# Delta rule with diagonal blocks of 32 rows, decay rows by turns on TensorE, and a new order of the front's steps

## The reference

```python
z = _rmsnorm(x, norm1_w) @ w_in           # q|k|v|gate|beta|decay of the delta rule, q|k|v of the attention
qkv = silu(causal_conv4(z[qa, ka, va]))   # 4 heads x 128
qa, ka = l2norm(qa) * 128 ** -0.5, l2norm(ka)
g = -exp(a_log) * softplus(alpha + dt_bias); gc = cumsum(g)      # within a chunk
decay = exp(gc[i] - gc[j]) for i >= j
m = I + strictly_lower((k * beta) @ k.T * decay)
u, w = triangular_solve(m, [v * beta, k * beta * exp(gc)])
# per chunk: v_new = u - w @ S;  o = (q * exp(gc)) @ S + (q @ k.T * decay) @ v_new;  S = S * exp(gc_last) + k_dec.T @ v_new
ob = dilated_attention(qb, kb, vb, rel_bias)                     # 8 heads x 64, three branches
h = x + concat(gated_norm(o), ob) @ w_out
out = h + moe(_rmsnorm(h, norm2_w))       # top 4 of 32 experts, 1024 -> 2048 -> 1024
```

## Time and profile before

| | us |
|---|---|
| median of 3 runs (lowest, highest) | 1085.33 (1084.62, 1086.16) |
| span of the profiled execution | 1083.5 |
| TensorE busy | 1019.8 (94%) |
| VectorE busy | 303.6 (28%) |
| ScalarE busy | 164.3 (15%) |
| HBM read and written | 427 MB, 394 GB/s over the span |
| mean granted clock of TensorE | 0.990 |

### The profile page before, as it was taken

How to read it: one execution, slowest core, us unless ns; L and a number is a source line. 1 busy time by engine, 2 the same in 40 slices (tenths; PEclk the granted TensorE clock), 3 DMA queues, 4 the chain that set the end, 5 groups by cost and what they waited for, 6 DMA issues and landing times.

```text
span 1083.5 us, 12842 instructions
## 1 busy us (share of the span) xinstructions
PE 1019.8 (94%) x5096; PEld 447.5 (41%) x5096; DVE 303.6 (28%) x703; ACT 164.3 (15%) x283; POOL 21.3 (2%) x37
## 2 busy tenths in 40 slices
PE   9999999999999999989999989988999898988898
PEld 7888866333434343434344323232333332223232
DVE  4987754312222222222322111101111111111111
ACT  3513436011111111111001000000111011111101
POOL 3201000000000000000000000000000000000000
PEclk9999999999999999999999999999999999999999
DMA  9724779999999999999999999999999999999997
GB/s 324 283 83 161 279 287 365 405 425 428 425 419 432 434 432 428 432 432 429 428 432 428 427 429 431 431 432 429 431 431 431 431 431 430 431 431 434 425 424 289
DMA packets 39036, 427.64 MB, mean 395 GB/s; under 512 B 8251, under 2 KB 10524, under 8 KB 20188
## 3 DMA queue, kind: packets, MB, share of 16 engines
q1 hardware_dynamic: 37840, 426.84, 93.9%
q10 hardware_dynamic: 1164, 0.34, 0.1%
HBM read 424.42 MB, written 2.75 MB: 394 GB/s over the span
## 4 chain that ended last, share of the span: by engine, by line
PE 50%; DMA 41%; DVE 5%; issue 1%; ACT 1%; SPq 1%; ACTq 0%; DVEq 0%
DMA store<-in_w_gate_up_dram 24%; PE bank L2312 17%; DMA store<-in_w_down_dram 16%; PE bank L2370 13%; PE bank L1789 5%; PE bank L1781 3%; PE bank L2218 2%; PE bank L1916 2%; PE bank L2077 2%; PE bank L2283 1%; DVE flow L1627 1%; PE bank L2335 1%; DVE flow L1620 1%; ACT flow L1010 1%; DVE flow L1625 1%
## 5 line engine op out<-in xcount | busy, mean ns | idle before, releaser
L2312 PE MATMUL bank<-store,flow 128*64 128x512 f32 x2048 | 452.0, 598 | 13.9 <-DMA store<-in_w_gate_up_dram 12.9
L2312 PEld LDWEIGHTS bank<-store,flow 128*64 128x64 f32 x2048 | 145.9, 138 | 314.1 <-issue 289.9
L2370 PE MATMUL bank<-store,flow 128*64 128x512 f32 x992 | 228.1, 610 | 32.1 <-DMA store<-in_w_down_dram 20.5
L1620 DVE TENSOR_SCALAR flow<-bank 128x512 f32<-128x512 f32 x32 | 22.1, 692 | 607.8 <-PE bank L2312 607.8
L2370 PEld LDWEIGHTS bank<-store,flow 128*64 128x64 f32 x992 | 74.0, 140 | 165.5 <-issue 138.4
L1010 ACT ACTIVATE flow<-flow 128x512 f32<-128x512 f32 x32 | 20.2, 630 | 445.0 <-DVE flow L1620 445.0
L2227 PE MATMUL bank<-qkT 64*128 64x512 f32 x248 | 61.9, 616 | 0.0
L1026 ACT COPY qkT<-bank 128x512 f32<-128x512 f32 x31 | 18.2, 586 | 194.6 <-PE bank L2370 194.6
L1020 ACT COPY flow<-flow 128x512 f32 x30 | 33.7, 1124 | 27.5 <-DVE flow L1695 11.2
L2227 PEld LDWEIGHTS bank<-qkT 64*128 64x128 f32 x248 | 21.2, 186 | 40.1 <-issue 40.1
L1781 PE MATMUL bank<-store 128*128 128x256 f32 x160 | 35.5, 381 | 0.0
(11 more groups left out here) (360 smaller groups left out, 671.0 us busy)
## 6 DMA issues: line engine op xcount, KB each, us to landing
store<-in_w_gate_up_dram SPq DMA_DIRECT2D x50, 4096.0 KB, 26.9
store<-in_w_down_dram SPq DMA_DIRECT2D x57, 2048.0 KB, 20.9
store<-in_w_gate_up_dram SPq DMA_DIRECT2D x26, 2048.0 KB, 13.8
store<-in_w_in_dram SPq DMA_DIRECT2D x6, 2048.0 KB, 13.7
store<-in_w_down_dram SPq DMA_DIRECT2D x9, 1024.0 KB, 25.0
store<-in_w_out_dram SPq DMA_DIRECT2D x1, 4096.0 KB, 14.3
store<-in_w_gate_up_dram SPq DMA_DIRECT2D x3, 1024.0 KB, 7.2
flow<-in_w_down_dram SPq DMA_DIRECT2D x1, 2048.0 KB, 11.9
```

The source lines that it names most:

```text
L1620: dve.tensor_scalar(gt, bank[4][:], LIMIT, None, ALU.min).then_inc(g_min, 1)
L2312: ins = mm(dst[SLOTS * hf:SLOTS * (hf + 1), :], rows[:, c:c + SLOTS], store[:, slot_at(j, odd) + c0:slot_at(j, odd) + c0 + 512], start=fir ...
L2370: ins = mm(dst[SLOTS * hf:SLOTS * (hf + 1), :], turned[:, c:c + SLOTS], w[:, hf * 512:(hf + 1) * 512], start=f == 0, stop=f == KT - 1)
```

## The change

- Diagonal blocks of 32 rows: `n_cols` and `t_cols` have 32 columns a head, the masks follow. Each of the 32 blocks is loaded four times, to 128 partitions; every partition inverts the two 16x16 halves on its diagonal (`invert_halves`, step J0), and then (`join_halves`, step J1) picks the four columns of the halves that are its own, and computes the lower left part as a product of the two inverses and the block's lower left.
- The series has the powers of D up to the third: stage Q, the product X and ScalarE's copy in stage 7, and the product Y and its copy in stage 8 are gone. Stages 8 and 9 of tile 1 use bank 6 and not bank 4.
- The decay rows are the column of the cumulative decay, broadcast as the stationary operand and turned by the identity, one turn a head. `ug` and its eight instructions are gone; TensorE waits for the cumulative decay itself.
- The first tap of each convolution is a scaled copy on ScalarE (`first_tap`) behind its `evac`. The first convolution stands before the decay's inputs, the sums of x before the decay; the quarter sums of piece 4 go to GpSimd and those of piece 3 to VectorE; the sixth convolution and q's sums are now steps V6 and Q0 of the order, behind 01 and 11, and `g5` stands in front.
- A new order.

```diff
-FINE = 16
-BLOCKS = 64
+FINE = 32
+HALF = FINE // 2
+BLOCKS = 32
+PARTS = 4
...
-BY_POOL = {3: 3}
-SUMMED_BY = {("b", 3): ("sums", 0), ("d", 3): ("sums", 1), ("b", 4): ("sums", 2), ("c", 4): ("sums", 3),
+BY_POOL = {4: 3}
+SUMMED_BY = {("b", 3): ("sums", 1), ("c", 3): ("sums", 2), ("d", 4): ("sums", 3),
...
-    text = ("01 11 a3 a4 b3 b4 g5 u5 c3 c4 h5 J0 d3 d4 r0 12 e4 02 0E e3 1E r1 a5 r2 n0 17 07 f0 b5 f1 f2 g6 "
-            "08 f3 c5 S0 d5 09 S1 P0 0A P1 e5 S2 h6 T0 0B a6 u6 O0 0Q P2 b6 0C T1 S3 c6 O1 1K T2 d6 P3 0M e6 "
-            "s0 S4 O2 18 P4 0N T3 W0 T4 19 O3 1A 0D O4 S5 P5 1B W1 T5 1Q O5 w0 X0 1C X1 W2 1M A0 1N H0 H1 R0 "
-            "1D L0 W3 F0 X2 G0 M0")
+    text = ("g5 01 11 Q0 V6 a3 a4 b3 b4 h5 J0 c3 c4 d3 d4 J1 e4 e3 r0 r1 u5 r2 a5 0E 1E 02 n0 b5 12 17 07 f0 f1 08 "
+            "c5 f2 f3 09 S0 d5 0A S1 P0 g6 e5 0B S2 P1 h6 T0 0C a6 u6 O0 1K T1 P2 b6 O1 S3 18 c6 T2 P3 19 d6 O2 1A "
+            "e6 s0 0M S4 T3 P4 1B W0 0N O3 1C T4 S5 P5 0D O4 W1 1M T5 w0 X0 1N O5 X1 A0 W2 1D H0 H1 R0 W3 L0 F0 X2 "
+            "G0 M0")
...
-            sp.dma_start(n_sq, by_block(n_dram)).then_inc(ld_blocks, 16)
+            sp.dma_start(n_sq, bass.AP(n_dram.tensor, 0, [[0, PARTS], [FINE * FINE, BLOCKS], [1, FINE * FINE]])
+                         ).then_inc(ld_blocks, 16)
             sp.wait_ge(t_ready, 1)
-            sp.dma_start(by_block(t_dram), t_sq).then_inc(st_scratch, 16)
+            sp.dma_start(bass.AP(t_dram.tensor, 0, [[PARTS * FINE, PARTS], [FINE * FINE, BLOCKS],
+                                                    [HALF * FINE, 2], [1, PARTS * FINE]]),
+                         t_own.rearrange("q (a n) -> q a n", a=2)).then_inc(st_scratch, 16)
...
+            def first_tap(u):
+
+                act.wait_ge(z_evac, evacuated(u))
...
+                for c in (CONV_AT[u], CONV_AT[u] + 1):
+                    tp.mark(act.activation(conv[:, c, :], zpad[:, c, 0:S], ACT.Copy, scale=cw[:, 0, c:c + 1]))
...
-            def invert_blocks():
+            def invert_halves():
 
                 dve.wait_ge(ld_blocks, 16)
...
+                for j in range(1, HALF - 1):
+                    shape = [P, 2, j, HALF - 1 - j]
+                    part = t_new[:, 0:2 * j * (HALF - 1 - j)].rearrange("q (a c r) -> q a c r", a=2, c=j)
+                    st.step(dve.tensor_tensor(part, n_diag[:, :, j + 1:HALF, j].unsqueeze(2).to_broadcast(shape),
+                                              t_of[:, :, 0:j, j].unsqueeze(3).to_broadcast(shape), ALU.mult))
+                    st.step(dve.tensor_tensor(t_of[:, :, 0:j, j + 1:HALF], t_of[:, :, 0:j, j + 1:HALF], part,
+                                              ALU.add))
+
+            def join_halves():
...
+                def product(rows, cols):
+                    shape = [P, PARTS, HALF, HALF]
+                    part = t_new.rearrange("q (c r k) -> q c r k", c=PARTS, r=HALF)
+                    st.step(dve.tensor_tensor(part, rows.unsqueeze(1).to_broadcast(shape),
+                                              cols.unsqueeze(2).to_broadcast(shape), ALU.mult))
+                    return part
+
+                st.mark(dve.memset(own_second[:, :, 0:HALF], 0.0))
+                picked = own_halves.rearrange("q (a m) -> q a m", a=2)
+                st.step(dve.tensor_scalar(picked, columns(0), part_of[:, 0:1], None, ALU.mult))
+                for g in range(1, PARTS):
+                    st.step(dve.scalar_tensor_tensor(out=picked, in0=columns(g), scalar=part_of[:, g:g + 1],
+                                                     in1=picked, op0=ALU.mult, op1=ALU.add))
+                st.mark(dve.tensor_copy(own_diag, own_halves.rearrange("q (a c r) -> q a c r", a=2, r=HALF)))
+                first = own_halves[:, 0:PARTS * HALF].rearrange("q (c r) -> q c r", r=HALF)
+                st.step(dve.reduce_sum(low_right, product(n_low, first), AX_X))
+                Tally(dve, t_ready).mark(dve.reduce_sum(
+                    own_first[:, :, HALF:], product(t_of[:, 1].rearrange("q k r -> q r k"), low_right), AX_X))
...
                     elif s == 8:
-                        st.step(dve.tensor_copy(m["F"], Y[:]))
-                        gdn.mark(dve.tensor_copy(m["V"], Z[:]))
+                        gdn.mark(dve.tensor_copy(m["V"], W[:]))
...
+            pe.wait_ge(gap_ready, 1)
             for t in range(T):
 
-                pe.wait_ge(ug_ready, HG * (t + 1))
-                gr.mark(mm(bank[t][:], ones[:], ug[:, t, :], start=True, stop=True))
+                for h in range(HG):
+                    ins = mm(bank[t][:, h * P:(h + 1) * P], gd[:, 5, t, h:h + 1].to_broadcast([P, P]), ident[:],
+                             start=True, stop=True, is_transpose=True)
+                gr.mark(ins)
...
                     elif s == 7:
-                        product(X, m["G"], m["L"])
                         ins = product(Y, m["L"], m["G"])
...
                     elif s == 8:
-                        product(Y, m["N"], m["D"])
-                        ins = product(Z, m["G"], m["H"])
+                        ins = product(W, m["G"], m["H"])
```

More of the change, by code:

```diff
@@ L91 @@
 ORDER = attention_order()
-PE_STAGES = {1, 2, 7, "K", 8, 9, 10, 11, "Q", 12, 13}
+PE_STAGES = {1, 2, 7, "K", 8, 9, 10, 11, 12, 13}
 DVE_STAGES = PE_STAGES | {"E", "M", "N"}
-ACT_STAGES = {7, "M", "N"}
+ACT_STAGES = {"M", "N"}
 EARLY_STAGES = {1, 2, 7}
-BANK4_STAGES = {2, 8, 9}
-BANK4 = [step for step in ORDER if (step[0] == "gdn" and step[2] in BANK4_STAGES) or step[:2] == ("a", 6)]
+BANK4_STAGES = {(0, 2), (1, 2), (0, 8), (0, 9)}
+BANK4 = [step for step in ORDER if (step[0] == "gdn" and step[1:] in BANK4_STAGES) or step[:2] == ("a", 6)]
 BANK7 = [step for step in ORDER if step[0] in "TO"]
@@ L1202, in _ @@
             convolve(1)
+            dve.wait_ge(ba_psum, 1)
+            dve.wait_ge(ld_small, 16 * 8)
+            ba = bank[3][:, 0:T * 2 * HG].rearrange("p (t n) -> p t n", t=T)
+            st.mark(dve.tensor_scalar(gd[:, 4], ba[:, :, 0:HG], -1.0, None, ALU.mult))
+            dd.mark(dve.tensor_tensor(gd[:, 3], ba[:, :, HG:2 * HG],
+                                      gd[:, 1, 0].unsqueeze(1).to_broadcast([P, T, HG]), ALU.add))
+            dd.mark(dve.tensor_scalar(col[:, 17:18], col[:, 17:18], DH ** -0.5, None, ALU.mult))
+            sums_of_x()
             dve.wait_ge(dec_act, 2)
@@ new lines, in join_halves, with columns @@
+            def join_halves():
+                def columns(g):
+                    return t_of[:, :, PARTS * g:PARTS * (g + 1), :].rearrange("q a c r -> q a (c r)")
+                def product(rows, cols):
[15 more added lines that the diff above has]
+                    own_first[:, :, HALF:], product(t_of[:, 1].rearrange("q k r -> q r k"), low_right), AX_X))
@@ L1357, in _ @@
                 if kind == "J":
-                    invert_blocks()
+                    (join_halves if a else invert_halves)()
+                    continue
+                if kind == "V":
+                    convolve(a)
+                    continue
+                if kind == "Q":
+                    Tally(dve, q_sums).step(picked_sums(2, gd[:, 9]))
+                    st.step(dve.tensor_scalar(gd[:, 9], gd[:, 9], EPS, EPS * DK * DK, ALU.add, ALU.mult))
                     continue
@@ L2069, in _, with product @@
                         pe.wait_ge(z_sum, sums_done("e", 5))
[L2070 removed]
+                    if (t, s) == (1, 12):
                         pe.wait_ge(z_evac, evacuated("d6"))
                     take_shared((kind, t, s))
[L2074 removed]
+                    def product(dst, lhsT, rhs):
                         for h in range(HG):
```

136 lines of the change are left out of this document (62 added, 74 removed).

## The result

The changed kernel takes 1109.88 us (median of 4 runs, 1108.75 to 1112.6) where the kernel before took 1085.07 in the same session: a ratio of 1.0229, 95% interval 1.0214 to 1.0245. It is slower, as forecast, but by 24.8 us where 9.2 were forecast, and it lies outside the range (1083 to 1100).

What follows compares the result with a forecast made beforehand. TensorE bounds the front, streamed bytes the rest. Seven waits of 17.2 us, less 6.2 of removed TensorE work, 1.8 of small gaps and 0.1, give 9.2 on 1085.3: 1094.5 us, range 1083 to 1100.

Steps and rivals of the forecast that it cites:

- removed work decides: Rival: VectorE keeps up, waits stay under 6.2 us and TensorE's removed work makes it faster, 1079.1 us; chance 0.16.
- The DMA hides it: Rival: the DMA is already short of time at 160 to 180 us, late block 0 costs nothing, 1085.3; chance 0.08.
- the first trip: Loading the blocks through DRAM ahead of J0, four times the bytes: 0.8 us more, ends 0 and 3.
- The second trip: Storing the inverses and loading their columns after J1: nothing added to the time of before.
- (1): ScalarE's last silu waits for VectorE's sixth convolution and q's sums behind 01 and 11, delaying b3: 1.6 us.
- (2): TensorE waits before stage 02, listed behind 0E, which needs the inverse's columns, back at 91.5: 2.7 us.
- (3): Stage 12 stands behind n0 on VectorE, so stage 17 starts late, and f1 and S0 wait for copies: 2.4 us.
- (4): Before stage 0C, VectorE needs 7.9 us for its steps since 0A while TensorE has 4.5 of work: 3.2 us.
- (5): T1 waits for O0, which stands behind a6's copy and u6: 1.2 us.
- (6): 0M stands behind s0, so VectorE starts S4 late and O3, 1C and T4 come late: 2.4 us.
- (7): W1 needs the bank that 0D empties, queued on VectorE behind P5, which needs ScalarE's exps: 3.7 us.
- The clock: Rival: TensorE's clock falls behind idle gaps at two waits, 1.2 us or a little more each, 1097; chance 0.17.

Runs made afterwards that it cites:

- loads: The changed kernel with the load that replicates the blocks four times split into four transfers of 32 partitions; 1103.94 us (ratio 1.0164).
- twos: The changed kernel with the load of the blocks as two transfers of two copies each; 1113.62 us (ratio 1.025).
- best5: As hold, with step h5 moved behind r2 and c5 put between f0 and f1; 1086.99 us (ratio 1.0008).
- pool: As loads, with GpSimd's four squares held until the end of J1; 1101.44 us (ratio 1.0148).
- straight: As pool, with the second half inverse copied once so J1's second product reads no strided operand; 1102.53 us (ratio 1.0149).
- trips: As loads, with the store of the inverses also split into four transfers of 32 partitions; 1103.1 us (ratio 1.016).
- late: The changed kernel with three steps moved earlier in the list (g6 ahead of 09, 0M ahead of e6, 0D ahead of S5); 1097.77 us (ratio 1.011).
- hold: As best3, with the copy of straight and two weight loads held until the columns' load has landed; 1087.39 us (ratio 1.0016).
- only0d: The changed kernel with one step moved, 0D ahead of S5; 1102.85 us (ratio 1.015).
- warm: The changed kernel with 59 dummy products of the unit matrix put into three of TensorE's idle times; 1104.46 us (ratio 1.0169).
- best3: The changed kernel with the edits of loads, pool and late, u6 behind O0, and 02, 12, b5, u5 placed anew around the inverse; 1089.29 us (ratio 1.0027).

## Why the prediction was right or wrong

**The sign and the mechanism** were right. The waits that VectorE's order makes for TensorE decide, and the later start of block 0 (206.1 for 183.2) arrives in the total, with 1.9 us more on top. The rival "removed work decides" fell: idle time in the front was 21.5 us, not under 6.2. "The DMA hides it" fell too.

**The steps up to 69 us** were right to 0.4: the last projection unit ends 0.7 earlier (0.75 forecast), blocks leave at 64.35 (64.0), b3 starts at 68.9 (68.7).

**The term that failed first is the first trip** ("0.8 more for the first trip, ends 0 and 3"). It was priced by its bytes; it took 6.5 more (8.7 for 2.1). 4.6 of them come from an access pattern whose outer dimension of four engaged four engines (loads, twos): split, the same bytes took 4.1 (best5). J0 began at 75.2, not 70.7. The kernel's rows before gave no price for this shape; but its outer dimension could have been counted, and the Trainium skill's page named under twos has the rule, which the prediction did not draw on. With the load split, J0 starts at 70.70 as forecast.

**J0** was 9.2 for 8.8, **J1** 8.6 for 6.8. Without GpSimd beside it (1.3) and the strided operand (0.7) J1 would be 6.6 (pool, straight); the rows it was priced by had neither. **The second trip** took 5.7 for 4.5; its store has an outer dimension of four too, but splitting it won nothing (trips).

**The waits by their numbers**, forecast and found: (1) 1.6 and 1.57; (2) 2.7 and 7.82, with e4's 2.34 beside it, which the list had not foreseen; (3) 2.4 and 1.22; (4) 3.2 (its own terms, 7.9 less 4.5, give 3.4) and 2.67; (5) 1.2 and 0.87; (6) 2.4 and 1.59; (7) 3.7 and 3.44. Waits 4 to 7, 10.5 by forecast, were 8.6; late took 7.2 of them away and left T1, T4 and 0.16 at 0C. The whole miss of wait 2 is the inverse's.

**The clock** was the second step that failed: the sum puts it at nothing, and a rival adds 2.4 us for it. It came on top: three falls, 1.7 to 2.7 us each instead of 1.2, together 6.3. It should have been a term of the sum: the forecast had three waits of 2.7 and more, and the row it cited, a wait of 2.76, had the fall behind it. The Trainium skill's "TensorE: Matmul & The Clock Gate", section "HAM oscillation", says that a long enough gap in TensorE's work throttles it, so that the next products start cold. The trace agrees for the three long waits (2.67 to 7.82 us).

**The sum at X1**: forecast 9.3 later, found 22.9. The difference of 13.6 is 4.3 of waits (21.5 less 17.2), 6.3 of clock, and 3.0 that the prediction has under small gaps. Of these 1.8 is its third wrong term: it took off 1.8 us of gaps in the kernel before, and that trace has 0.4 us of them (PE busy 96.92 us, in the columns of the earlier trace rows):

```profile
57.28:154.60 97.32, 96.92 (x589) 79.84 (x586) 69.35 (x150) 31.47 (x73) 4.46 (x4) 1.00 0.55 204
```

The other 1.2 lies in how a wait is read. The modelled ends of products overlap the next row, so each of the eleven waits costs 0.07 to 0.17 us more from start to start than the idle time in its bracket; T1 starts 2.03 us behind the row before it, where that step took 0.99 before, and its bracket says 0.87.

**What the change could have given.** 6.2 us less TensorE work is real (the decay rows' share was seen, 0.9). Against it stands a chain of trip, J0, J1 and trip that takes 29.1 us (hold) to 35.2 (the changed kernel) from the blocks' store to the columns where it took 18.5 before (67.0 to 85.53). Covered as well as any list tried covers it, it leaves TensorE idle for about what was saved (5.3 us in hold, whose X1 starts at 154.65 for 154.60), and the time is that of the kernel before.

## What to carry to other kernels

Where a change puts a new transfer on a chain, count the outermost dimension of its pattern before its bytes: one transfer with four copies as its outer dimension took 8.7 us where four transfers of 32 rows took 4.1. Where the order of work is one list for all engines, look for steps on a helper engine that stand just ahead of what TensorE needs, and give each long wait a second term for the slow products behind it, which in the changed kernel came to 1.7 to 2.7 us a wait. Measure such a list with single moves: the one measured alone here was worth 7.0 us and the three together 12.1, where the arithmetic that the change removed is 6.2.

## What the runs showed that I had not expected

- Two transfers with an outer dimension of two ran on the same two engines and were slower (13.9 us) than one of four (8.7).
- That one transfer of four copies took 8.7 us in the changed kernel's profile and 9.3, 10.2 and 9.7 in those of late, only0d and warm, which do not touch it.
- The same wait has the clock fall in one run and not in another: behind the 2.67 us at 0C the products took 2.77 us in the changed kernel, 2.05 in trips and pool, 2.87 in loads. Behind the 2.44 at f1 it fell in best3 and not in hold, and it did not fall behind 2.96 at e4 in late. Behind the 3.44 at W1 it fell in all six profiles that have this wait, for 5.40 to 6.56 us of products instead of 3.70. The length of the wait alone does not settle it, and what does is open.
- A 128x128 step of VectorE took 0.94 instead of 0.23 us beside a 128x512 product on GpSimd.
- The load of 1024 short rows for the columns took 2.3 to 3.9 us in profiles that have the same transfer; best3 and best5, where stage 17 waits for it, spread over 4.1 and 4.6 us in 10 and 11 runs, but hold over 2.3 in 10, and the kernel before over 3.3 in 21. No experiment here was on its cause, which stays open.
